# Interleaved experts, and a final gather in two halves: one inference step of a hybrid encoder with a mixture of experts

## The reference

```
lg    = xf @ w_router_group + b_router_group           # 4 groups
g_sel = argmax(lg);  p_sel = softmax(lg)[g_sel]
le    = (xf @ w_router_expert)[g_sel] + b_router_expert  # 4 experts of the chosen group
top_v, top_i = top_k(softmax(le), 2)
gates = p_sel * top_v / sum(top_v)
a = silu(xf @ w_gate[e]) * (xf @ w_up[e]) * combine[:, e]   # for each of 16 experts, FF = 256
y = sum over e of a @ w_down[e];   out = h + y
```

## Time and profile before

| | us |
|---|---|
| median of 3 runs (lowest, highest) | 518.95 (517.83, 521.62) |
| the profiled execution, whole | 517.57 |
| its span | 515.8 |
| busy: PE, DVE, ACT, POOL | 445.1, 294.9, 251.2, 176.8 |
| expert steps (about) | 331 to 485, later ones 9.6 us apart |
| last store of expert rows issued, landed | 485.4, 488.9 |
| first and last of the ten gathers issued | 491.0, 503.5 |
| last output store issued | 513.5 |

### The profile page before, as it was taken

The page is one execution under the profiler, slowest core; times in us unless marked ns, Lnnn a source line. Parts: engine busy times, 40 slices in busy tenths (PEclk is TensorE's granted clock), DMA queues, the critical chain, the costliest instruction groups (busy, mean ns, idle before and its releaser), DMA issues. The chain is left out here.

```text
span 515.8 us, 7224 instructions
## 1 busy us (share of the span) xinstructions
PE 445.1 (86%) x2569; PEld 329.5 (64%) x2569; DVE 294.9 (57%) x442; ACT 251.2 (49%) x360; POOL 176.8 (34%) x179
## 2 busy tenths in 40 slices
PE   5999999999798999999999941799999999999400
PEld 4877877787586666667777841566666666666200
DVE  3535442354633645562333747358998998998236
ACT  4664333563424636462115521457877877877100
POOL 0384000514200000001003741137767767745270
PEclk9999999999979999999999985789999999999955
DMA  8872222222214000001695695269999999994376
GB/s 254 214 245 84 88 83 81 83 83 102 100 49 169 1 1 1 1 0 42 212 361 175 216 376 183 82 237 326 338 341 304 348 340 340 356 350 169 97 251 268
DMA packets 63445, 94.78 MB, mean 184 GB/s; under 512 B 10592, under 2 KB 43360, under 8 KB 63408
## 3 DMA queue, kind: packets, MB, share of 16 engines
q1 hardware_dynamic: 54336, 69.87, 41.6%
q0 software_dynamic: 5088, 17.89, 10.8%
q10 hardware_dynamic: 3984, 6.56, 3.5%
HBM read 81.27 MB, written 13.04 MB: 183 GB/s over the span
## 5 line engine op out<-in xcount | busy, mean ns | idle before, releaser
L1348 DVE TENSOR_TENSOR wlo<-raw,whi 128x2048 fp32r<-128x2048 f32 (+1 forms) x45 | 96.9, 2154 | 23.1 <-ACT whi L917 23.0
L1465 PE MATMUL bank<-whi,xT_hi 128*128 128x512 f32 x224 | 92.8, 414 | 2.7 <-DVE wlo L1015 2.1
L1466 PE MATMUL bank<-wlo,xT_hi 128*128 128x512 f32 x224 | 89.8, 401 | 0.0
L1467 PE MATMUL bank<-whi,xT_lo 128*128 128x512 f32 x224 | 89.6, 400 | 0.0
L917 ACT ACTIVATE whi<-raw 128x2048 fp32r<-128x2048 f32 x45 | 86.1, 1914 | 5.2 <-PE bank L1467 5.2
L622 POOL TENSOR_TENSOR wlo<-raw,whi 128x1024 fp32r<-128x1024 f32 x16 | 59.7, 3729 | 36.3 <-ACT whi L917 36.3
L1465 PE MATMUL bank<-whi,xsT_hi 128*96 128x512 f32 x128 | 53.8, 420 | 4.7 <-DVE xsT_lo L1354 3.5
L1465 PEld LDWEIGHTS bank<-whi,xT_hi 128*128 128x128 f32 x224 | 42.8, 191 | 14.3 <-issue 3.9
L1466 PE MATMUL bank<-wlo,xsT_hi 128*96 128x512 f32 x128 | 51.5, 403 | 0.0
L1467 PE MATMUL bank<-whi,xsT_lo 128*96 128x512 f32 x128 | 51.3, 401 | 0.0
L1467 PEld LDWEIGHTS bank<-whi,xT_lo 128*128 128x128 f32 x224 | 42.8, 191 | 10.5
(11 more groups left out here) (223 smaller groups left out, 774.6 us busy)
## 6 DMA issues: line engine op xcount, KB each, us to landing
raw<-in_w_gate_dram SPq DMA_DIRECT2D x32, 512.0 KB, 6.1
raw<-in_w_up_dram SPq DMA_DIRECT2D x32, 512.0 KB, 7.5
raw<-in_w_down_dram SPq DMA_DIRECT2D x32, 512.0 KB, 6.8
raw<-in_w_in_dram SPq DMA_DIRECT2D x9, 1024.0 KB, 5.2
expert_rows<-yout POOLq DMA_DIRECT2D x16, 384.0 KB, 5.3
raw<-in_w_out_dram SPq DMA_DIRECT2D x4, 1024.0 KB, 5.1
x_sb<-in_x_prompt_dram SPq DMA_DIRECT2D x8, 256.0 KB, 6.1
normed_tokens<-xn ACTq DMA_DIRECT2D x4, 512.0 KB, 2.9
```

Of the source, the lines that this page charges most:

```text
L1348: dve.tensor_tensor(wlo[SPLIT_OF[m3]][:, 0:n], eraw[slot][:, 0:n], whi[SPLIT_OF[m3]][:, 0:n].bitcast(F32), ALU.subtract).then_inc(m_lo, 1)
L1465: pe.matmul(acc, x_hi, w_hi, start=start, stop=False)
L1466: pe.matmul(acc, x_hi, w_lo, start=False, stop=False)
L1467: return pe.matmul(acc, x_lo, w_hi, start=False, stop=stop)
```

## The change

Experts run in another order, interleaved over the groups: position p of the order holds expert p // 4 of group p % 4. A token's two experts belong to one group, so they run at least four positions apart, and the one that runs first stands in positions 0 to 11. The rows in `expert_rows` lie by position. DVE sorts each token's two choices by position (`choices_by_place`: the lower into choice 0, the gates with them) after expert 2. The five gathers of the choice that runs first move: three into POOL's order after lo(14), ahead of store(12), two after lo(15), ahead of store(13). Ahead of the first of them POOL waits for the splits of units 0 to 40 (whose buffers it overwrites) and for the stores of experts 0 to 11. The five gathers of the other choice come after the last store and ahead of reading the flag. DVE first adds the five tiles of the first choice, then the five of the second. If the flag is set the rows are fetched again at the end. Cut to its core:

```diff
+    FIRSTS = (E - NG) * CAP
+        early_y = [sb(f"early_y{i}", [P, NT], I32) for i in range(2)]
-        sel = [sb(f"sel{i}", [P, NT, NG, EPG], stack=st_c) for i in range(2)]
+        sel = [sb(f"sel{i}", [P, NT, EPG, NG], stack=st_c) for i in range(2)]
...
+        def expert_at(j, b):
+            return EPG * (b % NG) + j + b // NG
...   SP: every load takes its expert from expert_at, as here
-                    gate_up_unit(i, 1, m, 3 * b)
+                    gate_up_unit(expert_at(j, b), 1, m, 3 * b)
...   POOL: end of moe_gathers
-                for i in range(E - 1 - BODY, E):
+                for i in range(E - 1 - BODY, E - 2):
                     step(i, 0, 0, i % 2)
+                lo(E - 2, 0, 0)
+                if isinstance(r, int):
+                    pool.wait_ge(places_ok, 1)
+                    pool.wait_ge(m_hi, 3 * (E - NG) + NT)
+                    pool.wait_ge(m_lo, 3 * (E - NG) + NT)
+                    for p in range(2):
+                        pool.wait_ge(y_st[p], 16 * (E - NG) // 2)
+                    for t in range(3):
+                        fetch(0, t)
+                store(E - 4, 0)
+                lo(E - 1, 0, 0)
+                if isinstance(r, int):
+                    for t in range(3, NT):
+                        fetch(0, t)
+                store(E - 3, 1)
                 lo(E, 0, 0)
                 store(E - 2, 0)
                 store(E - 1, 1)
...
+            def fetch(c, t, pos=early_y, n=(FIRSTS, SLOTS)):
+                pool.indirect_dma_start(yg[c][t][0:rows[t], :], None, y_dram[0:n[c], :],
+                                        bass.IndirectOffsetOnAxis(ap=pos[c][0:rows[t], t:t + 1], axis=0))\
+                    .then_inc((yg_second if c else yg_first)[t], 16)
             moe_gathers(0)
+            for t in range(NT):
+                fetch(1, t)
             pool.wait_ge(flag_ok, 1)
             more = pool.value_load(flag[0:1, 0:1], min_val=0, max_val=1)
             with pool.If(more != 0):
...
-                fetch(ROUNDS * SLOTS)
-            with pool.Else():
-                fetch(SLOTS)
+                for t in range(NT):
+                    for c in range(2):
+                        fetch(c, t, pos_y, (ROUNDS * SLOTS, ROUNDS * SLOTS))
...   DVE: sel is written in the order (expert, group); the places end in eid
-                link(dve.tensor_tensor(sel[c][:, :, :, :], gb, eb, ALU.mult))
+                link(dve.tensor_tensor(sel[c][:, :, :, :].rearrange("p t e g -> p t g e"), gb, eb, ALU.mult))
...
-                ins = dve.scalar_tensor_tensor(out=pos_y[c][:, :], in0=rd[:, :], ...
+                link(dve.scalar_tensor_tensor(out=eid[:, :], in0=rd[:, :], ...
+            def choices_by_place():
+                p0, p1, later, sooner = r1[8], r1[9], r1[10], r1[11]
+                low, high = r1[6], r1[7]
+                dve.tensor_tensor(low[:, :], p0[:, :], p1[:, :], ALU.min)
+                link(dve.tensor_tensor(high[:, :], p0[:, :], p1[:, :], ALU.max))
+                for c, (pos, n) in enumerate(((low, FIRSTS), (high, SLOTS))):
+                    dve.tensor_copy(pos_y[c][:, :], pos[:, :])
+                    ins = dve.tensor_scalar(early_y[c][:, :], pos[:, :], float(n - 1), None, ALU.min)
+                ins.then_inc(places_ok, 1)
+                dve.tensor_tensor(later[:, :], p0[:, :], p1[:, :], ALU.is_gt)
+                link(dve.tensor_tensor(sooner[:, :], p0[:, :], p1[:, :], ALU.is_le))
+                for c in range(2):
+                    same, other = (sooner, later) if c == 0 else (later, sooner)
+                    dve.tensor_tensor(r1[2 * c][:, :], gate[0][:, :], same[:, :], ALU.mult)
+                    link(dve.tensor_tensor(r1[2 * c + 1][:, :], gate[1][:, :], other[:, :], ALU.mult))
+                for c in range(2):
+                    ins = dve.tensor_tensor(gate[c][:, :], r1[2 * c][:, :], r1[2 * c + 1][:, :], ALU.add)
+                link(ins)
...   in moe, after step 2
+                if isinstance(r, int):
+                    choices_by_place()
...
+            def add_rows(n):
+                for c, ld in enumerate((yg_first, yg_second)):
+                    for t in range(NT):
+                        p = rows[t]
+                        dve.wait_ge(ld[t], 16 * n)
+                        if c:
+                            dve.wait_ge(first_added, t + 1)
+                        dve.scalar_tensor_tensor(out=x_sb[0:p, t, :], in0=yg[c][t][0:p, :], scalar=gate[c][0:p, t:t + 1],
+                                                 in1=x_sb[0:p, t, :], op0=ALU.mult, op1=ALU.add).then_inc(y_ok if c else first_added, 1)
...
             with dve.If(more != 0):
...
+                add_rows(2)
+            with dve.Else():
+                add_rows(1)
```

More of the change, by code:

```diff
@@ L64, in trunk_step @@
     AHEAD = 2
-    assert FF * 2 == CB and D == 2 * CB and HEADS * HD == CB and SEQ == CB and E == 16
+    assert BODY == NG and FF * 2 == CB and D == 2 * CB and HEADS * HD == CB and SEQ == CB and E == 16
     xn_dram = nc.dram_tensor("normed_tokens", [TOK, D], F32, kind="Internal").ap()
@@ L240, in trunk_step @@
         y_st = [sem(f"y_st{i}") for i in range(2)]
-        yg_ld = [sem(f"yg_ld{t}") for t in range(NT)]
+        yg_first = [sem(f"yg_first{t}") for t in range(NT)]
+        yg_second = [sem(f"yg_second{t}") for t in range(NT)]
+        first_added = sem("first_added")
         y_ok, y_out = sem("y_ok"), sem("y_out")
@@ L423, in raw_free, with gate_up_unit, down_unit @@
                         sp_.sem_inc(sp_tick, 1)
-                def gate_up_unit(i, half, m, slot):
+                def gate_up_unit(e, half, m, slot):
                     raw_free(m)
-                    load_gate_up(i, half, slot)
-                def down_unit(i, m, slot):
+                    load_gate_up(e, half, slot)
+                def down_unit(e, m, slot):
                     raw_free(m)
-                    load_down(i, slot)
+                    load_down(e, slot)
                 def first(m):
@@ L443, in first @@
                     if m < 2:
-                        gate_up_unit(0, m, m, m)
+                        gate_up_unit(expert_at(0, 0), m, m, m)
                     elif (m + 1) % 3 == 2:
-                        down_unit(i - 1, m, m)
+                        down_unit(expert_at(0, i - 1), m, m)
                     else:
-                        gate_up_unit(i, (m + 1) % 3, m, m)
+                        gate_up_unit(expert_at(0, i), (m + 1) % 3, m, m)
                 def few_in_flight(i, b, c):
@@ L455, in few_in_flight, with step @@
                     sp_.sem_inc(sp_tick, 1)
-                def step(i, b):
+                def step(j, b):
+                    i = BODY * j + b
                     m = 3 * i
                     few_in_flight(i, b, 0)
-                    gate_up_unit(i, 1, m, 3 * b)
+                    gate_up_unit(expert_at(j, b), 1, m, 3 * b)
                     few_in_flight(i, b, 1)
@@ L464, in step @@
                     sp_.sem_inc(sp_tick, 1)
-                    down_unit(i - 1, m + 1, 3 * b + 1)
+                    down_unit(expert_at(j, b - 1), m + 1, 3 * b + 1)
                     few_in_flight(i, b, 2)
-                    gate_up_unit(i + 1, 0, m + 2, 3 * b + 2)
+                    gate_up_unit(expert_at(j, b + 1), 0, m + 2, 3 * b + 2)
                 for m in range(NRAW):
@@ L472, in moe_loads @@
                     for b in range(BODY):
-                        step(BODY * j + b, b)
+                        step(j, b)
                 for b in range(BODY - 1):
-                    step(E - BODY + b, b)
-                gate_up_unit(E - 1, 1, 3 * E - 3, NRAW - 3)
+                    step(E // BODY - 1, b)
+                gate_up_unit(expert_at(0, E - 1), 1, 3 * E - 3, NRAW - 3)
                 sp_.wait_ge(m_lo_pool, (E + 1) * r + E - 4)
                 sp_.sem_inc(sp_tick, 1)
-                down_unit(E - 2, 3 * E - 2, NRAW - 2)
-                down_unit(E - 1, 3 * E - 1, NRAW - 1)
+                down_unit(expert_at(0, E - 2), 3 * E - 2, NRAW - 2)
+                down_unit(expert_at(0, E - 1), 3 * E - 1, NRAW - 1)
             moe_loads(0)
@@ L485, in _ @@
             with sp_.If(more != 0):
+                for t in range(NT):
+                    sp_.wait_ge(yg_first[t], 16)
+                    sp_.wait_ge(yg_second[t], 16)
                 with sp_.Fori(1, ROUNDS) as r:
@@ L1268, in _ @@
             link(dve.tensor_reduce(le[:, :, :], r16[:, :, :, :].rearrange("p t g e -> p t e g"), AX.X, ALU.add))
-            tmp4 = sel[0][:, :, 0, :]
             link(dve.tensor_copy(r16[:, :, 0, :], le[:, :, :]))
@@ L1278, in _ @@
                 eb = eoh[c][:, :, :].rearrange("p t (a e) -> p t a e", a=1).broadcast_to([P, NT, NG, EPG])
-                link(dve.tensor_tensor(sel[c][:, :, :, :], gb, eb, ALU.mult))
-            s2 = [s[:, :, :, :].rearrange("p t g e -> p t (g e)") for s in sel]
```

(9 more changed lines are left out.)

## The result

The changed kernel takes 516.43 us (median of 20 runs, among them one disturbed run of 760 us that the comparison leaves out), the kernel before 518.86, measured beside it: a ratio of 0.9947 (95% interval 0.9927 to 0.9966), 2.4 to 2.8 us less. The forecast was 9.1 less and a range of 506 to 514.5. The sign was right and the size a quarter of what was promised. The profiled execution took 516.32, its span 514.6, which is 1.2 less than the span of the profiled execution before.

What follows compares the result with a forecast made beforehand. PE was taken as full until 485 us, then an end of 26.9 us without PE, its gathers limited by data. Terms -1.5 - 9.4 + 0 + 1.4 + 0.4 = -9.1 gave 509.8 us, range 506 to 514.5.

Steps and rivals of the forecast that it cites:

- ahead of the sorting: Before DVE's sorting: added waits fall where DVE idles for the first tokens' gather, so they cost 0.
- sorting: DVE's fourteen short operations between steps 2 and 3: 1.8 us of work, mostly regained, +0.4 (0 to 1.8).
- three early gathers: POOL between lo(14) and store(12): three gathers of 0.95 hidden in 5.26 us of idling, 0.
- two later ones: Two gathers ahead of store(13) and lo(16): lo(16) pushed by 2.5, of which +1.4 delays PE's last down product.
- last store's landing: Landing of the last expert's store: the prediction's sum has no term for a change here.
- flag and branch: After the last store POOL goes straight to five gathers, without reading the flag first: -1.5 (0 to -2.0).
- from first late gather to end: Five gathers and one add per tile after the last store: 15.4 us instead of 24.8, -9.4.
- Rival C: Delays in front eat the gain: sorting costs its whole 1.8, lo(15) and lo(16) late, last tile later; 514.5, chance 0.14.
- Rival D: DVE's splits hold the early gathers, lo(16) ends at some 495; about 522.8, slower than before, chance 0.05.
- The order of experts: Interleaved experts: SP issues the same loads from the same queue, cost 0.

## Why the prediction was wrong, point by point

Each term against the two profiled executions. The right column adds up to -1.1; the spans differ by -1.2, and the rest is rounding.

| step | forecast | measured | from |
|---|---|---|---|
| ahead of the sorting | 0 | +0.7 | lo(3) at 348.88 and 348.15 |
| sorting | +0.4 | +2.0 | lo(14) at 465.87 and 463.17, less 0.7 |
| three early gathers | 0 | +1.5 on PE (lo(15) +3.0) | product 14 at 480.99 and 476.81, less 2.7 |
| two later ones | +1.4 | +1.8 | product 15 at 487.07 and 481.10, less 4.2 |
| last store's landing | 0 | +0.9 | 4.4 and 3.5 |
| flag and branch | -1.5 | -1.3 | 0.8 and 2.1 |
| from first late gather to end | -9.4 | -6.7 | 18.1 and 24.8 |

The first row is no effect that is known: lo(3) starts between 348.05 and 350.06 in the twelve profiled executions, whatever the kernel. By size the end missed most (2.7), then the sorting (1.6) and the three gathers (1.5). One mechanism that the sum has at nothing, the hold between DVE and POOL, stands behind the three gathers, has a part in the sorting and in the two later gathers, and made the first late landing 0.9 later.

**The three early gathers** are the step that failed in kind. I took them as hidden, with nothing late, pricing each from a gather of 0.94 beside a DVE split, of which I wrote: "The trace agrees for the copy and not for the 96-row gather." The runs showed 2.86, 3.10 and 1.42, and lo(15) 3.0 late. The row just above that gather had the answer: the index copy of 1.70 ends at 440.38, and the split beside it ends at the same moment (437.38 + 2.96 = 440.34). In the kernel before:

```profile
437.38 2.96 DVE L1348 TENSOR_TENSOR wlo<-raw,whi 128x2048 fp32r<-128x2048 f32 x1 [1.18 <-ACT whi L917]
...
441.19 0.40 DVE L1360 TENSOR_TENSOR sg<-sg,bank 96x256 f32<-96x256 f32 x1
```

The copy had already waited; the gather came 0.8 later, at 441.18, while DVE ran an operation whose other input is in PSUM (`bank`), and the split of 441.52 began 0.34 after it. A duration measured in a fixed rhythm holds for that place in the rhythm. Rival C, the nearest in time with 514.5, had the sorting at its whole 1.8 and some delay of the gathers. Rival D named the mechanism and its place rightly and got 0.05. Its price, 3.18 of waiting for each, was too high: the first and third gather met the rest of an operation (1.9 and 0.5 of waiting), the second a whole split, but one of 2.27, and of the two later ones only one met any. The Trainium skill (SBUF — State Buffer, who interferes with whom) says that a DVE instruction with two inputs in SBUF and a POOL instruction that reads SBUF contend for an interface that only one can have; the table above and the run with the splits in pieces agree, where the prediction had said that the trace did not for a gather. That the wait ends with one instruction agrees in the table, and not for the three gathers with 4.96, 3.34 and 7.19.

**PE's part of it.** The stretch of the last but one down product in the changed kernel (columns as in rows 2):

```profile
483.00:485.00 2.00, 2.00 (x6) 1.30 (x5) 0.00 (x0) 0.00 (x0) 1.94 (x3) 0.50 0.73 195
```

PE had idled 2.24 ahead of it; the granted clock is still 1.00 from 481 to 482 and 0.50 here, 1.2 GHz of 2.4: the product took 4.1 (480.99 to 485.08), 2.8 before. Little of that reached the end, since lo(16) was later still (486.85, against 486.53 for aT_lo).

**The sorting** was 2.0 for 0.4. I also put it one step too early (at 348 instead of 358), which changed nothing; what mattered was POOL's split, which I counted as a help (DVE's next split would be shorter) and not as a hold: the first operation stood until POOL was done, and the fourteen took 3.6 (358.57 to 362.16) for the 1.6 of the run with the early sorting. That run shows that the place costs 2.0; it takes away both the hold and the operations' own time, so how the 2.0 falls on the two is not shown.

**The end** was mis-sized by 2.7. DVE's adds in the changed kernel:

```profile
502.00 1.28 DVE L1466 SCALAR_TENSOR_TENSOR x_sb<-raw,gate,x_sb 128x1024 f32<-128x1024 f32 x1 [4.27 <-DMA raw<-expert_rows,early_y]
504.23 1.29 DVE L1466 SCALAR_TENSOR_TENSOR x_sb<-raw,gate,x_sb 128x1024 f32<-128x1024 f32 x1 [0.94 <-DMA raw<-expert_rows,early_y]
506.02 1.28 DVE L1466 SCALAR_TENSOR_TENSOR x_sb<-raw,gate,x_sb 128x1024 f32<-128x1024 f32 x1 [0.50 <-DMA raw<-expert_rows,early_y]
508.51 1.28 DVE L1466 SCALAR_TENSOR_TENSOR x_sb<-raw,gate,x_sb 128x1024 f32<-128x1024 f32 x1 [1.21 <-DMA raw<-expert_rows,early_y]
510.22 1.27 DVE L1466 SCALAR_TENSOR_TENSOR x_sb<-raw,gate,x_sb 32x1024 f32<-32x1024 f32 x1 [0.43 <-DMA raw<-expert_rows,early_y]
```

The first landing came at +5.5 instead of +4.6 (the first adds, which I had called hidden, held its gather), the others 2.2, 1.8 and 2.5 apart, near the 2.3 that the forecast has for gathers beside output stores, the small tile was waited for as well, and the last output store left 3.1 before the end instead of 2.3: 0.9, 0.6, 0.4 and 0.8. Why the last store took longer, and why the gathers kept the slower pace, is not shown. The order of experts cost nothing that can be measured, as forecast, and the flag term was right. The mechanism of the gain was right: one add per tile and half the gathers behind the last store, 6.7 less there, and 5 us net by the run with all gathers at the end.

## What to carry to other kernels

Before work is moved into an engine's idle time, look at what the engine that can hold it runs in that time: here POOL's idle time beside DVE's splits was not free (2.86, 3.10), and its idle time beside a DVE without such operations was (0.95 to 1.01). A short operation in a trace says little about a place where it would start at another moment; look for a neighbour of it that has already done the waiting. And a transfer that is moved ahead of the last store should be out of the DMA engines by then: that store took 6.9 with three gathers just ahead of it and 3.7 with the small one alone.

## What the runs showed of the hardware that was not expected

Small operations are not a sure remedy for the hold: with splits in pieces three gathers took 1.26, 1.11 and 0.94, but a gather issued 2.8 us into a row of twenty adds of 256 columns was held for 6.2 (7.19 less 0.95), through the rest of the row and the whole add behind it, where one issued 1.9 into the five whole adds of the run with two splits in pieces was in after 0.5 (1.46). The hold shows on POOL's gathers and splits and not on its plain stores: 0.53 for a store issued beside a DVE split, 0.51 beside none. And a store of 384 KB issued behind 1.1 MB of gathers took 6.9 us by the same queue and 7.6 by another engine's queue, 3.5 with nothing ahead of it.
